# Sums of squares of 256-wide heads: VectorE adds each head's two tiles, TensorE multiplies half as much

## The reference, cut to what matters

```python
def memory_cross_attention_branch(q, gate, mem_h, w_mem_kv, qn_g, kn_g, w_proj):
    k, v = jnp.split(mem_h @ w_mem_kv, 2, axis=-1)
    q = rms_norm(q.reshape(B, S, X_HEADS, X_HEAD_DIM), qn_g)      # X_HEAD_DIM = 256
    k = rms_norm(k.reshape(B, M, X_HEADS, X_HEAD_DIM), kn_g)
    s = jnp.einsum("bshd,bmhd->bhsm", q, k).astype(jnp.float32) * (X_HEAD_DIM ** -0.5)
    ...

def rms_norm(x, g, eps=1e-6):
    y = xf * lax.rsqrt(jnp.mean(xf * xf, axis=-1, keepdims=True) + eps)
    ...
```

## Time and profile before

| what | value |
|---|---|
| median of 3 runs | 1284.18 us (1283.8 to 1284.25) |
| profiled execution, its own time | 1284.4 us |
| its span | 1282.4 us |
| PE busy over the span | 1127.3 us, 88% |
| DVE busy | 969.6 us, 76% |
| ACT busy | 567.8 us, 44% |
| POOL busy | 559.3 us, 44% |
| line L474 (the products that are changed) | 32 MATMUL rows, 7.6 us busy |

### The profile page before, as it was taken

One profiled execution on the slowest core, in us unless ns is written; L12 is line 12 of the kernel. 1 busy time (PEld: TensorE's weight loads), 2 busy tenths in 40 slices (PEclk: granted clock), 3 DMA queues, 4 the chain that ended last, 5 costly groups with the idle time before them and its releaser, 6 DMA issues.

```text
span 1282.4 us, 15649 instructions
## 1 busy us (share of the span) xinstructions
PE 1127.3 (88%) x5606; PEld 779.8 (61%) x5606; DVE 969.6 (76%) x1962; ACT 567.8 (44%) x1038; POOL 559.3 (44%) x544
## 2 busy tenths in 40 slices
PE   6999999999989997999579887898778987777887
PEld 6989898999979997977335332353223532222322
DVE  5589989866789665677798876877768777777654
ACT  5476768654436435696423322422224222222221
POOL 0099999999300000000345544344445543434331
PEclk9999999999989998999899999899999999999999
DMA  7645444444554545625699999999999999999996
GB/s 256 213 133 165 131 145 138 146 140 157 165 196 163 179 160 166 197 99 195 242 419 424 428 427 427 395 427 426 427 427 398 427 424 427 427 428 426 421 427 265
DMA packets 127646, 374.37 MB, mean 292 GB/s; under 512 B 6864, under 2 KB 82640, under 8 KB 94672
## 3 DMA queue, kind: packets, MB, share of 16 engines
q0 software_dynamic: 36864, 268.45, 49.9%
q1 hardware_dynamic: 88496, 100.67, 24.0%
q10 hardware_dynamic: 2208, 4.24, 1.0%
HBM read 372.29 MB, written 1.05 MB: 291 GB/s over the span
## 4 chain that ended last, share of the span: by engine, by line
PE 52%; DMA 23%; DVE 15%; ACT 4%; issue 4%; SPq 0%; DVEq 0%; POOLq 0%; ACTq 0%
DMA big<-in_experts,big 18%; PE unit L728 12%; PE unit L420 11%; PE unit L422 11%; PE unit L421 11%; DVE work L1858 3%; DVE w_lo L1434 2%; DMA row<-in_experts,big 2%; DMA conv_in<-in_experts,big 2%; DVE big L1777 1%; ACT L836 1%; DVE conv_acc L1457 1%; DVE big L1774 1%; ACT probs L1177 1%; DVE big L1870 1%
## 5 line engine op out<-in xcount | busy, mean ns | idle before, releaser
L420 PE MATMUL unit<-in_hi,w_hi 128*128 128x256 f32 x1184 | 359.7, 304 | 2.7 <-DVE in_lo L1521 2.7
L421 PE MATMUL unit<-in_lo,w_hi 128*128 128x256 f32 x1184 | 336.6, 284 | 0.0
L422 PE MATMUL unit<-in_hi,w_lo 128*128 128x256 f32 x1184 | 336.6, 284 | 0.0
L1177 ACT ACTIVATE probs<-ident,big 128x128 f32<-128x128 f32 x256 | 102.8, 402 | 444.7 <-DVE big L1870 444.7
L728 PE MATMUL unit<-row,probs 128*128 128x512 f32 x512 | 249.3, 619 | 47.2 <-ACT probs L1177 47.0
L1434 DVE TENSOR_TENSOR w_lo<-w_raw,w_hi 128x2048 fp32r<-128x2048 f32 x91 | 210.5, 2319 | 70.9 <-ACT w_hi L845 70.7
L420 PEld LDWEIGHTS unit<-in_hi,w_hi 128*128 128x128 f32 x1184 | 228.9, 193 | 16.6 <-issue 14.7
L421 PEld LDWEIGHTS unit<-in_lo,w_hi 128*128 128x128 f32 x1184 | 228.9, 193 | 12.3 <-issue 12.0
L728 PE MATMUL unit<-big,probs 128*128 128x512 f32 x384 | 187.8, 622 | 48.7 <-ACT probs L1177 48.7
L422 PEld LDWEIGHTS unit<-in_hi,w_lo 128*128 128x128 f32 x1184 | 228.6, 193 | 0.0
L845 ACT CAST w_hi<-w_raw 128x2048 fp32r<-128x2048 f32 x91 | 172.7, 1903 | 105.7 <-PE unit L422 68.1
(11 more groups left out here) (256 smaller groups left out, 1341.6 us busy)
## 6 DMA issues: line engine op xcount, KB each, us to landing
w_raw<-in_w_in SPq DMA_DIRECT2D x58, 1024.0 KB, 5.2
w_raw<-in_w_mem_kv SPq DMA_DIRECT2D x8, 1024.0 KB, 5.2
w_raw<-in_w_out SPq DMA_DIRECT2D x8, 1024.0 KB, 5.1
w_raw<-in_w_query SPq DMA_DIRECT2D x6, 1024.0 KB, 5.3
w_raw<-in_w_diff_proj SPq DMA_DIRECT2D x4, 1024.0 KB, 5.3
w_raw<-in_w_x_proj SPq DMA_DIRECT2D x4, 1024.0 KB, 5.0
w_raw<-in_w_conv_proj SPq DMA_DIRECT2D x4, 1024.0 KB, 5.1
row<-in_experts,big POOLq DMA_INDIRECT x128
```

The costliest lines, as they stand in the source:

```text
L420: e.matmul(unit[:, to], *hi_hi, start=first, stop=False)
L421: e.matmul(unit[:, to], *hi_lo, start=False, stop=False)
L422: m = e.matmul(unit[:, to], *lo_hi, start=False, stop=final)
L1177: e.activation(diag_places[g % 12], ident[:, :], ACT.Copy, scale=here).then_inc(*mark("diag", g))
```

## The change

`head_sums` no longer multiplies four tiles of a 256-wide slot. Ahead of it VectorE adds tile 1 to tile 0 and tile 3 to tile 2, writes the sums to the first 512 columns of the same buffer, and TensorE multiplies those in one product of 512 columns. The new step of VectorE, `pair_squares`, stands first between the two low parts of the turn, behind two taps and ahead of `diff_probs`.

```diff
             def head_sums(name, place=None):
                 sq, unit = work.ap(name), units.take(name + " sums", place)
-                for wait in W(("sq", name), units.free(name + " sums"), ("const", None)):
-                    e.wait_ge(*wait)
                 per_head, dim = HEAD_NORMS[name][2:]
+                for wait in W(("sq" if per_head == 1 else "paired", name),
+                              units.free(name + " sums"), ("const", None)):
+                    e.wait_ge(*wait)
                 weights = ones64 if dim == 64 else ones
-                if per_head == 1:
-                    for g in range(2):
-                        m = e.matmul(unit[:, g * 512:(g + 1) * 512], weights[:, :],
-                                     sq[:, g * 512:(g + 1) * 512], start=True, stop=True)
-                else:
-                    for g in range(2):
-                        for j in range(2):
-                            a = 2 * g + j
-                            m = e.matmul(unit[:, g * T:(g + 1) * T], weights[:, :],
-                                         sq[:, a * T:(a + 1) * T], start=j == 0, stop=j == 1)
+                for g in range(2 // per_head):
+                    m = e.matmul(unit[:, g * 512:(g + 1) * 512], weights[:, :],
+                                 sq[:, g * 512:(g + 1) * 512], start=True, stop=True)
                 m.then_inc(*mark("sums", name))
...
+            def pair_squares(name):
+
+                sq = work.ap(name)
+                for wait in W(("sq", name)):
+                    e.wait_ge(*wait)
+                e.tensor_tensor(sq[:, 0:T], sq[:, 0:T], sq[:, T:2 * T], ALU.add).then_inc(
+                    *mark("pair_step"))
+                for wait in W(now("pair_step")):
+                    e.wait_ge(*wait)
+                e.tensor_tensor(sq[:, T:2 * T], sq[:, 2 * T:3 * T], sq[:, 3 * T:4 * T],
+                                ALU.add).then_inc(*mark("paired", name))
+
...
+                if pending in HEAD_NORMS and HEAD_NORMS[pending][2] == 2:
+                    norms.insert(0, partial(pair_squares, pending))
                 ahead(s, between=norms, convolve=3 if n < 4 else 2 if n < 16 else 4)
```

More of the change, by code:

```diff
@@ L461, in head_sums @@
                 sq, unit = work.ap(name), units.take(name + " sums", place)
-                for wait in W(("sq", name), units.free(name + " sums"), ("const", None)):
+                per_head, dim = HEAD_NORMS[name][2:]
+                for wait in W(("sq" if per_head == 1 else "paired", name),
+                              units.free(name + " sums"), ("const", None)):
                     e.wait_ge(*wait)
-                per_head, dim = HEAD_NORMS[name][2:]
                 weights = ones64 if dim == 64 else ones
-                if per_head == 1:
-                    for g in range(2):
-                        m = e.matmul(unit[:, g * 512:(g + 1) * 512], weights[:, :],
-                                     sq[:, g * 512:(g + 1) * 512], start=True, stop=True)
-                else:
-                    for g in range(2):
-                        for j in range(2):
-                            a = 2 * g + j
-                            m = e.matmul(unit[:, g * T:(g + 1) * T], weights[:, :],
-                                         sq[:, a * T:(a + 1) * T], start=j == 0, stop=j == 1)
+                for g in range(2 // per_head):
+                    m = e.matmul(unit[:, g * 512:(g + 1) * 512], weights[:, :],
+                                 sq[:, g * 512:(g + 1) * 512], start=True, stop=True)
                 m.then_inc(*mark("sums", name))
```

## The result

In the first comparison the changed kernel took 1287.66 us (median of 12 runs, 1284.67 to 1288.94) against 1283.91 us for the kernel before on the same chip. The ratio is 1.0027, 95% interval 1.0019 to 1.0035: slower by 0.27%, or 3.5 us (the medians stand 3.75 us apart; the ratios of this document are the record's own and differ from the quotients of the medians by up to 0.06%). That is just over the 0.2% that can be told from no change. The prediction was 1286.4 us, 2.3 us more than before with 0.1 taken off, and its range ended at 1287.8.

What follows compares the result with a forecast made beforehand. VectorE's chain in turns 7 to 10 was taken to decide when TensorE goes on: 3 x 1.4 - 1.91 = 2.3 us later, 1284.18 + 2.3 = 1286.5, lowered 0.1 to 1286.4 us; range 1284.4 to 1287.8 us.

Steps and rivals of the forecast that it cites:

- TensorE's saving: TensorE's sums in turns 7 to 10: 0.87 us less a turn, 3.5 us in all, reaching time only through VectorE.
- The bound of 1.91 us for free adds: VectorE from 177.34 in turn 7: it can lose only its waits of 1.53 and 0.38 us, the most gain possible.
- the prediction's own side remark: Turn 8: ScalarE's root could come only 0.87 us earlier than 192.61, at 191.74, with TensorE's whole saving from turn 7.
- VectorE loses its waits and then every add is paid: Turns 8 to 10: three pairs of adds lie on VectorE's chain, less 1.91 us of waits, 2.3 us later.
- The term d: Cost of one pair of VectorE adds on the chain in turns 8 to 10: 1.4 us, between 0.81 and 1.79.
- the lower bound of 0.81: Cheapest pair of VectorE adds, unhindered by GpSimd: 0.42 + 0.04 + 0.35 us; gives +0.5 us, 1284.7.
- Rows 7: Turn 7 trace rows: four larger diff_probs steps take 2.65 us; a GpSimd add beside VectorE's low part takes 2.85 us.
- The prediction's worst case: By the skill page's port lock, an add waits for a whole GpSimd add, putting a pair above 1.79 us.
- the new wait at the sums: TensorE's sums wait for the second add; in turn 10 this only moves the wait at diff_turn, 0.65 us further on.
- the shift reaches the end: Behind 234.04: TensorE's delay of 2.3 us passes on whole, through the meeting at 373.81, with no slack found.
- the three calls: Whole kernel time against 0.2%, 2.57 us: faster 0.04, same 0.63, slower 0.33.
- rival (c): Turns 8 to 10: GpSimd catches each add, a pair costs from 1.5 us, up to +3.5 us, 1287.6; chance 0.33.

Runs made afterwards that it cites:

- products_only: Changed kernel's single 512-column product without the adds, against the kernel before: 1281.35 us, ratio 0.9982, against 1283.68 us.
- taps_after: Changed kernel with eight of VectorE's convolution taps moved from turns 7-10 to 12-15, against the kernel before: 1284.68 us, ratio 1.0003.

## Why the prediction was right, and where it was off

- **That TensorE's saving can't come out: right.** `products_only` kept 0.68 us of 3.5. The bound of 1.91 us for free adds held; the prediction's own side remark, that the root of turn 8 comes only 0.87 us earlier, makes it 1.25, and 1.20 us of waits went. That VectorE is the engine to look at is right as well; that the two were level at 234.04 is not quite, since TensorE lost 0.65 us to VectorE in turns 10 and 11 and not 0.30.
- **That VectorE loses its waits and then every add is paid: right.** Its work from one `head_scale` to the next was 15.27 - 1.53 = 13.74, 15.27 - 0.38 = 14.89 and 14.73 us before, and is 14.63, 16.14 and 16.11 after: +0.89, +1.25 and +1.38, together 3.52. Less the waits of 1.91 that is 1.61 us, just what `diff_turn` of turn 10 shows.
- **The term d was mis-sized.** Taken at 1.4 us, it measured 3.52 / 3 = 1.17, which moves +2.3 to +1.6 us. Its make-up was other than said. Each add was to take 0.6 to 0.75 us, hindered by GpSimd; they took 0.41 and 0.50, and the pair 0.87, close to the lower bound of 0.81. A middle price of 1.4 is one that no pair had: the other kernels show 0.87 or 1.5 by the step of GpSimd in front, and the changed kernel has the cheap case in all of its eight pairs in two profiles. Rows 7, from which the price was built, were also read a little wrong: GpSimd's add from 170.92 on ends at 173.77, not with the low part (173.18) but 0.59 us behind it. What came on top of the pairs, 0.4 and 0.5 us in the two later turns, lay in unchanged steps. `diff_probs` of turn 9 took 203.73 - 200.61 = 3.12 us before and 204.82 - 201.38 = 3.44 after, and `head_scale` of turn 9 took 1.59 us up to the next step before, and 2.04 after. These are the first row of that `diff_probs` and the low part behind it, before and after:

```profile
200.61 0.16 DVE L1587 RECIPROCAL col<-col 128x4 f32<-128x4 f32 x1
...
203.73 2.28 DVE L1434 TENSOR_TENSOR w_lo<-w_raw,w_hi 128x2048 fp32r<-128x2048 f32 x1
```

```profile
201.38 0.17 DVE L1593 RECIPROCAL col<-col 128x4 f32<-128x4 f32 x1
...
204.82 2.28 DVE L1428 TENSOR_TENSOR w_lo<-w_raw,w_hi 128x2048 fp32r<-128x2048 f32 x1
```

That these steps took longer because they met GpSimd at another point is argued from the rows, not isolated by a run.
- **The Trainium skill's rule.** "SBUF — State Buffer" says, in its section "SBUF: two separate sides", that of a VectorE instruction with two SBUF inputs and a GpSimd instruction that reads SBUF, whichever starts first holds the shared port for its whole length, and that the other is blocked. Where VectorE came first the trace after agrees: a product of GpSimd that started at 182.01, 0.04 us behind a low part of 2.28 us, took 2.59 us, and the others there 0.48 to 0.92. Where GpSimd came first it agrees in part. A product did not hold up an add that came 0.22 us later (185.46 and 185.68) and grew itself. An add did (`taps_after`, 214.71 and 214.82), and VectorE lost 0.54 us by it, of the 0.68 that the other had left. The prediction's worst case, a pair above 1.79 us, came nowhere; the dearest took 1.51.
- **That the new wait at the sums moves and adds nothing: right in turn 10,** where it was 0.15 us. In turn 8, of which the prediction didn't speak, it was 0.71 us, and was made good at `diff_turn` behind it.
- **That the shift reaches the end: right up to 375 us, unsettled behind.** The two comparisons, of medians 3.75 and 2.1 us apart, lie on both sides of the predicted +2.3, the first only 0.14 us inside the range; the mean of all 23 runs of the changed kernel is 1286.5, 2.5 above the 1284.0 that lie between the two medians of before. So the time came out nearer to the forecast than the term that it was made of, and that is luck: the sum was 0.7 us too large for these turns, and what came up behind turn 11 made up for it, 2.1 us in the first comparison and 0.4 in the second by the medians, which no account explains. Of the three calls, the first comparison met slower (0.33) and the second the same (0.63). It met slower without the mechanism of rival (c), since no pair of the changed kernel cost 1.5 us.
- **What was missed** is the loop. It changed no number here, because the row (14.7 to 14.9 us a turn), the loop (30.41 for two) and TensorE's own work (29.94 for the same two) stood so close together before the change, but it decides what a remedy can do: from +1.6 us, moving the taps alone gave 1.7 us, moving the adds alone gave 0.6 by turn 10 (and lost 1.3 behind it with TensorE's clock), and both together gave 3.6, down to -2.0.

## What to carry to other kernels

When an engine waits in a loop, follow the result that it waits for back through every engine until the same step of an earlier turn comes up: work on that cycle costs, work beside it is free only as long as its own engine's row has room. Halving work on the engine that looks fullest brought 0.3 us a turn at best, because a cycle and a second engine's row stood within half a microsecond a turn of it, and because small shifts changed what steps cost that nobody had touched; here moving steps that were already there was worth more than the change itself. And for effects of a microsecond in 1284, compare landmarks in two traces from a common start, look at the granted clock between them before giving a difference to a wait, and run the unchanged kernel again as a yardstick, before reading anything into the total.

## What the runs showed of the hardware

- A pair of 128 x 256 adds on VectorE, the second waiting for the first, took 0.41 and 0.50 us, 0.87 up to the next step, in 22 of 29 pairs, in which a product of GpSimd had begun 0.21 to 0.23 us before. It took 1.5 us up to the next step in the six in which an add of GpSimd had begun 0.10 or 0.11 us before. One add over the same 512 columns in strided pieces delayed by 0.60 us, and once by 1.15.
- A shift of VectorE's steps against GpSimd's goes with other prices of steps that were not touched: 2.16 or 2.61, 3.12 or 3.44 us for one `diff_probs`, 1.59 or 2.04 for one `head_scale`.
- After one and the same pause TensorE's granted clock stayed at 0.50 for 3.4 us in one profile of an unchanged program and for 10.2 us in another; with the rest that came of it, two profiles that agree to 0.01 us up to 345 us end 2.3 us apart.
- In one profile of 14 the clock fell to 0.50 at 222 us behind a wait of only 1.96 us, with TensorE busy for 3.60 of the 5 us up to 220, and about 1.6 us were lost by it.
